# A mixture-of-experts stage: the last expert list as code of its own, its side work on DVE, and a deeper run ahead

## The reference

```python
def block_fn(args):
    tok, e = args                       # at most 128 rows of one expert
    xb = xf[tok]
    return (jax.nn.silu(xb @ w1[e]) * (xb @ w3[e])) @ w2[e]
...
y = y * gate_buf[:, None].astype(y.dtype)
out = jax.ops.segment_sum(y, tok_buf, num_segments=n)
...
e = jax.nn.sigmoid(h @ ple_gate_w[i] + ple_gate_b[i]) * (p[i] @ ple_w[i])
h = layer_norm(DEEPNORM_ALPHA * h + f + e, ln2_g[i], ln2_b[i])
```

## Time and profile before

| | |
|---|---|
| median of 3 runs | 2218.81 us (2215.59 to 2225.62) |
| the profiled execution | 2218.86 us |
| its span in the trace | 2217.1 us |
| instructions executed | 30503 |
| PE busy | 2142.3 us, 97% |
| PE weight loads busy | 1745.6 us, 79% |
| DVE busy | 1556.5 us, 70% |
| ACT busy | 1270.9 us, 57% |
| POOL busy | 175.5 us, 8% |
| 381 loads of expert chunks | 4.8 us each, median from issue to landing |

### The profile page before, as it was taken

One profiled execution on the slowest core, in us unless ns is written; L12 is line 12 of the kernel. 1 busy time (PEld: TensorE's weight loads), 2 busy tenths in 40 slices (PEclk: granted clock), 3 DMA queues, 4 the chain that ended last, 5 costly groups with the idle time before them and its releaser, 6 DMA issues.

```text
span 2217.1 us, 30503 instructions
## 1 busy us (share of the span) xinstructions
PE 2142.3 (97%) x11389; PEld 1745.6 (79%) x11389; DVE 1556.5 (70%) x1331; ACT 1270.9 (57%) x1270; POOL 175.5 (8%) x157
## 2 busy tenths in 40 slices
PE   9999999999999999999999999999999999999987
PEld 8977797877867999875777887878787878878765
DVE  6766544556246555635888888888888888888798
ACT  6755443333344333333677777676777776777655
POOL 0021010000202100200500000000000000000240
PEclk9999999999999999999999999999999999999999
DMA  6522594223835555543699999999999999999985
GB/s 224 185 95 91 178 349 158 71 76 115 262 128 198 182 186 190 161 148 114 233 406 360 376 367 370 377 361 369 368 366 369 368 357 380 365 370 368 357 321 230
DMA packets 85884, 584.56 MB, mean 264 GB/s; under 512 B 10016, under 2 KB 10016, under 8 KB 19504
## 3 DMA queue, kind: packets, MB, share of 16 engines
q1 hardware_dynamic: 76160, 547.91, 65.9%
q0 software_dynamic: 9184, 34.54, 4.4%
q10 hardware_dynamic: 464, 1.02, 0.1%
HBM read 563.06 MB, written 15.73 MB: 261 GB/s over the span
## 4 chain that ended last, share of the span: by engine, by line
PE 84%; DVE 6%; DMA 3%; ACT 2%; issue 2%; POOL 1%; ACTq 0%; POOLq 0%; DVEq 0%; SPq 0%
PE bank L582 75%; DVE wrest L2372 2%; DMA arena<-arena 2%; DMA ring<-in_w_moe 1%; PE bank L1294 1%; ACT whi L1737 1%; POOL arena L498 1%; PE bank L786 1%; PE bank L918 1%; PE bank L813 1%; DVE h L2123 1%; PE bank L1102 1%; PE bank L916 1%; PE bank L1120 0%; PE bank L895 0%
## 5 line engine op out<-in xcount | busy, mean ns | idle before, releaser
L2372 DVE TENSOR_TENSOR wrest<-ring,whi 128x2048 fp32r<-128x2048 f32 x381 | 869.9, 2331 | 97.0 <-ACT whi L1737 94.8
L1737 ACT ACTIVATE whi<-ring 128x2048 fp32r<-128x2048 f32 x378 | 703.8, 1918 | 83.7 <-DMA ring<-in_w_moe 81.3
L582 PE MATMUL bank<-whi,xgT 128*128 128x512 f32 x1008 | 406.7, 403 | 20.2 <-DVE wrest L2372 20.1
L582 PE MATMUL bank<-wrest,xgT 128*128 128x512 f32 x1008 | 397.2, 394 | 0.0
L582 PE MATMUL bank<-whi,xgR 128*128 128x512 f32 x1008 | 394.7, 392 | 0.0
L582 PEld LDWEIGHTS bank<-whi,xgT 128*128 128x128 f32 x1008 | 190.2, 189 | 66.7 <-DVE wrest L2372 26.5
L582 PEld LDWEIGHTS bank<-whi,xgR 128*128 128x128 f32 x1008 | 190.2, 189 | 47.1
L582 PEld LDWEIGHTS bank<-wrest,xgT 128*128 128x128 f32 x1008 | 189.5, 188 | 39.1
L582 PE MATMUL bank<-whi,hidE 128*128 128x512 f32 x504 | 201.3, 399 | 9.5 <-DVE hidR L2377 5.5
L582 PE MATMUL bank<-wrest,hidE 128*128 128x512 f32 x504 | 198.0, 393 | 0.0
L582 PE MATMUL bank<-whi,hidR 128*128 128x512 f32 x504 | 196.7, 390 | 0.0
(11 more groups left out here) (426 smaller groups left out, 3757.5 us busy)
## 6 DMA issues: line engine op xcount, KB each, us to landing
ring<-in_w_moe SPq DMA_DIRECT2D x381, 1024.0 KB, 4.8
ring<-in_w_dense SPq DMA_DIRECT2D x135, 1024.0 KB, 4.9
row<-in_rows POOLq DMA_DIRECT2D x17, 512.0 KB, 7.6
xg_rows<-ncT POOLq DMA_DIRECT2D x12, 512.0 KB, 20.4
y_rows<-arena POOLq DMA_DIRECT2D x9, 512.0 KB, 6.7
arena<-xg_rows SPq DMA_DIRECT2D x9, 512.0 KB, 5.4
arena<-arena POOLq DMA_DIRECT2D x32, 142.0 KB, 7.4
arena<-in_tbias POOLq DMA_DIRECT2D x2, 1536.0 KB, 16.3
```

What stands on the lines that cost most here:

```text
L582: ins = pe.matmul(out_, lhsT, rhs, start=start, stop=stop, **more)
L1737: S["w_hi"].on(a.activation(whi[:, n % HI_SLOTS, :], ring[:, c % RING, :], ACT.Copy))
L2372: S["w_lo"].on(v.tensor_tensor(wrest[:, s, :], ring[:, s, :], whi[:, n % HI_SLOTS, :].bitcast(F32), ALU.subtract))
```

## The change

The loop runs over all lists but the last (`last_list`, a value of its own in `plan_i`), and the last list follows as a second copy of the body, with `last` true: without `turn_gathered`, the split of gathered rows and the chunks ahead. In it DVE does POOL's weighting and adding, four operations at chunks 20, 24, 28 and 32, and PE takes its last chunk bank by bank, so that bank 2 is complete first. `hidE` and `hidR` have two buffers, and turn 6 stands between the two chunks of `second(5)`. `AHEAD` is 4. PE's wait for the copied outputs stands in step 1. `embed(1)`'s six operations each wait until PE has begun a given chunk of list 0.

```diff
-AHEAD = 3
+AHEAD = 4
+EMBED_AT, Y_AT = (4, 8, 12, 15, 18, 21), (20, 24, 28, 32)
...
+        hidE = (rounded("hidE0", 6144, 4, P), rounded("hidE1", 20736, 4, P))
+        hidR = (rounded("hidR0", 24064, 4, P), rounded("hidR1", 21248, 4, P))
...
-            for k in range(AHEAD):
-                sp.wait_ge(chunks_used.sem, n * E_CHUNKS + (N_DENSE - RING + k + 1))
-                s = (FIRST_SLOT + k) % RING
-                sp.dma_start(ring[:, s, :], w_moe[k]).then_inc(ready[s], 16)
...
+                    if i:
+                        pool.wait_ge(chunks_used.sem, N_DENSE + EMBED_AT[3 * j])
                     S["ple_done"].on(pool.tensor_tensor(fe[:, j, :], fe[:, j, :], ppx[:, j, :], ALU.mult))
...
-            pool.wait_ge(moe_dma, n_iter * 16 + (SCATTERED + 64))
-            for n in range(4):
-                S["m_fe"].on(pool.tensor_tensor(yg[:, n, :], yg[:, n, :], weight[:, n:n + 1].to_broadcast([P, D]), ALU.mult))
-            for n in range(4):
...
-                S["m_fe"].on(pool.tensor_tensor(fe[:, n % 2, :], fe[:, n % 2, :], yg[:, n, :], ALU.add))
...
+                def second(j, between=None):
+                    wait(pe, "m_hr", i * E_STEPS + (j + 1))
                     for half in range(2):
+                        if half and between is not None:
+                            turn_hid(between)
                         wh, wr = expert_chunk(i, n[0], 2)
                         n[0] += 1
+                        if last and j == E_STEPS - 1 and half:
+                            for c in range(2):
...
+                                S["m_w2"].on(ins)
...
-                    if j == 0:
-
+                    if j == 1:
                         wait(pe, "m_ya", i + 1)
                         wait(pe, "m_yv", i + 1)
                         wait(pe, "pg_in", 8)
-                    else:
+                    if j:
                         turn_hid(j - 1)
                     wait(pe, "m_hid", i * E_STEPS + j)
                     columns(1, "m_h3")
                     if j:
-                        second(j - 1)
-                turn_hid(E_STEPS - 1)
-                turn_gathered(i)
+                        second(j - 1, j if j == E_STEPS - 1 else None)
+                if not last:
+                    turn_gathered(i)
                 second(E_STEPS - 1)
...
+            with pe.Fori(0, last_list) as i:
+                expert_list(i, False)
+            expert_list(last_list, True)
...
                 wait(a, "m_tr", i * E_STEPS + (j + 1))
-                wait(a, "m_w2", i * E_STEPS + j)
+                wait(a, "m_w2", i * E_STEPS + max(j - 1, 0))
...
-                for n in range(AHEAD, E_CHUNKS + AHEAD):
+                for n in range(AHEAD, E_CHUNKS + (0 if last else AHEAD)):
                     round_chunk(i, n)
-                    if n == 3:
+                    if n == AHEAD:
                         copy_outputs(i)
...
+                    if last and n in Y_AT:
+                        q = Y_AT.index(n)
+                        if q == 0:
+                            wait(v, "ple_done", 12)
+                            v.wait_ge(moe_dma, last_list * 16 + (SCATTERED + 80))
+                        if q >= 2:
+                            v.wait_ge(S["m_fe"].sem, q - 1)
+                        S["m_fe"].on(v.scalar_tensor_tensor(fe[:, q % 2, :], yg[:, q, :], weight[:, q:q + 1], fe[:, q % 2, :],
+                                                            ALU.mult, ALU.add))
```

More of the change, by code:

```diff
@@ L1269, in _, with expert_list @@
             wait(pe, "router_done", 1)
-            n_iter = pe.value_load(plan_i[0:1, 0:1], min_val=N_EXP, max_val=LISTS)
+            last_list = pe.value_load(plan_i[0:1, 1 + SECONDS:2 + SECONDS], min_val=N_EXP - 1, max_val=LISTS - 1)
             assert over[0] == 1
-            with pe.Fori(0, n_iter) as i:
+            def expert_list(i, last):
                 n = [0]
@@ L1295, in turn_hid @@
                     S["m_tr"].on(ins)
-                def second(j):
-                    wait(pe, "m_hr", i * E_STEPS + j + 1)
+                def second(j, between=None):
+                    wait(pe, "m_hr", i * E_STEPS + (j + 1))
                     for half in range(2):
+                        if half and between is not None:
+                            turn_hid(between)
                         wh, wr = expert_chunk(i, n[0], 2)
                         n[0] += 1
+                        if last and j == E_STEPS - 1 and half:
+                            for c in range(2):
+                                cs = slice(c * 512, (c + 1) * 512)
+                                for k in range(2):
+                                    ins = split_product(ps[2 + c][:, :], (hidE[j % 2][:, 2 + k, :], hidR[j % 2][:, 2 + k, :]),
+                                                        (wh[:, k, cs], wr[:, k, cs]), False, k == 1)
+                                S["m_w2"].on(ins)
+                            give(1)
+                            continue
                         for k in range(2):
@@ L1781, in _ @@
                         round_hid(i, E_STEPS - 1)
-                        wait(a, "m_h3", i * E_STEPS + E_STEPS)
-                        round_gathered(i + 1)
-            copy_outputs(n_iter)
+                        if not last:
+                            wait(a, "m_h3", i * E_STEPS + E_STEPS)
+                            round_gathered(i + 1)
+            with a.Fori(0, last_list) as i:
+                expert_list(i, False)
+            expert_list(last_list, True)
+            copy_outputs(last_list, 1, E_STEPS)
         @block.vector
@@ L2440, in _, with expert_list @@
             prime(v, "m_hid", "m_hr")
-            with v.Fori(0, n_iter) as i:
-                for n in range(AHEAD, E_CHUNKS + AHEAD):
+            def expert_list(i, last):
+                for n in range(AHEAD, E_CHUNKS + (0 if last else AHEAD)):
                     rest_chunk(i, n)
-                    if n == 3:
+                    if n == AHEAD:
                         copy_outputs(i)
@@ L2452, in _ @@
                         rest_hid(i, E_STEPS - 1)
-                        rest_gathered(i + 1)
-            copy_outputs(n_iter)
-            wait(v, "m_fe", 8)
+                        if not last:
+                            rest_gathered(i + 1)
+                    if last and n in Y_AT:
[7 more added lines that the diff above has]
+                                                            ALU.mult, ALU.add))
+            with v.Fori(0, last_list) as i:
+                expert_list(i, False)
+            expert_list(last_list, True)
+            copy_outputs(last_list, 1, E_STEPS + 1)
+            v.wait_ge(S["m_fe"].sem, 4)
             layer_norm(fe, row_of("ln2_g", 3), row_of("ln2_b", 2), add_last)
```

47 lines of the change are left out of this document (23 added, 24 removed).

## The result

| | before | after |
|---|---|---|
| median | 2220.31 us (2215.59 to 2225.62, 6 runs) | 2193.4 us (2190.6 to 2201.66, 6 runs) |
| ratio | | 0.9885, 95% interval 0.9864 to 0.9907 |
| profiled execution | 2218.86 us, span 2217.1 | 2192.72 us, span 2191.0 |

The change makes the kernel 1.1% faster. The forecast was 2190.4, and the range of 2181 to 2203 holds the result.

What follows compares the result with a forecast made beforehand. PE, with 84% of the chain, bounds the kernel, so time is only where it stands still or does unneeded work. 2.3 + 8.3 + 5.1 + 1.4 + 8.4 + 3.0 = 28.5 off 2218.9 gives 2190.4 us; range 2181 to 2203.

Steps and rivals of the forecast that it cites:

- Turn 6: Usual list ends: turning ahead of chunk 39 with two buffers saves 0.25 us of the 0.77 lost, 2.3 us in all.
- R1: DVE doesn't hold chunk 40, or GpSimd costs nothing in list 0: 4.6 and 2.5 us more, both 2183; chance 0.15.
- Four ahead, waits moved: List borders: PE's waits at chunk 2 of the next list go, 8.3 us at seven borders and 5.1 at the last.
- the 1.67 of the last border: Chunks 2 to 11 after the last border: 1.67 us over their work, read as a clock below full after the wait.
- List 0: First list: PE turns 3.9 us earlier, less 2.5 charged for GpSimd's six embedding operations; net gain 1.4 us.
- The scatters: List 0: the four queue behind GpSimd's last embedding operation, with 38 us left for issue and landing; nothing charged.
- The price of one GpSimd operation: Beside DVE's subtractions: 2.0 us lost for each, kept against 3.4 by the Trainium skill's exclusion rule.
- R2: List 0: GpSimd shuts DVE out, so the embedding costs 11 us, not 2.5, and 2199 results; chance 0.17.
- The last list: Adds moved from GpSimd to DVE: of 10.97 us lost, 2.6 stay, so 8.4 us are gained.
- the transfers' part: Last list: waits for ring chunks landing beside the gather still cost PE 2.2 us, bounds 0.9 and 5.
- R3: Transfers are full: usual borders give nothing back and the last list keeps 5 us, giving 2204; chance 0.08.
- R4: Last list's own code comes late to PE: x us per chunk loses 42x, 2232 at x = 1.0; chance 0.04.

## Why the prediction was right

**The path.** The forecast sat on PE's waits and DVE's queue, and five of six terms came within 0.2 us. The sum is 0.7 below what was measured, and the dense stages took 3.07 longer: 2190.4 - 0.7 + 3.1 = 2192.8, where the profiled execution took 2192.72. That the forecast met the median to 3.0 us, with runs 11 us apart, says less.

**Turn 6.** Right in mechanism and size: DVE's queue, not the turn, was next in line, and kept over half of the loss at chunk 40: 0.28 a list went with the double buffer, 0.58 with hidR's place. R1 with its 4.6 more was wrong as a forecast of this kernel, but its 4.6 was there to be had, by an order of DVE that the change doesn't have: that run's eight usual lists gave 8 x 0.58 = 4.6.

**Four ahead, waits moved.** Right in sum. The prediction priced them together and thereby hid how unequal they are. Given the moved wait, the fourth chunk adds 1.27 at most. Without it, four ahead are 47 slower than the pair, and at 1161.53 they are 17.8 slower than the kernel before (1143.73), although all the rest of the change is in. The miss of that run, 2241.67 for "near 2220", is one of its expectation and not of the prediction: it had the wait right and left out the clock behind it. The prediction did read such a loss into the 1.67 of the last border and into list 0, and granted clocks of 0.87 (2069.42 to 2082.18) and 0.88 bear it out. But "after a wait of over 3 us" is no rule: a wait of 3.32 in the run with the wait in step 0 cost no clock, and one of 2.24 in the run with the adds on GpSimd cost 1.3 us and 0.3 more in the next round. The changed kernel kept its clock behind the same 2.24, and so did all four of the other variants with a wait of 2.25 there. The prediction charged nothing for it and gave no reason; that much was luck, worth 1.6 us.

**List 0.** The net of 1.4 was measured as 2.71 - 1.31 = 1.40, and the parts are nearly right by luck. Not foreseen was the 0.68 at chunk 2, behind bias additions of DVE that its fourth subtraction pushes back (with three ahead it is gone); the three waits sum to 3.32, where 1.3, 1.4 and 1.0 for GpSimd had been worked out at chunks 4 and 5. The charge for the first operation, 1.0, is shown by the run without spacing (2.24 to 1.24). The second cost nothing, where 0.9 was charged, and those at chunks 15 and 21 cost 0.77 and 0.68 (rounds of 17.85 and 17.76), where 0.2 each was charged: 2.45 in sum for 2.5. The scatters, charged at nothing, cost what they did before, only later: 18.34 for one round, 18.49 before.

**The price of one GpSimd operation.** 2.0 was near enough, but the reason for keeping it was wrong. DVE's and GpSimd's rows in list 0 of the changed kernel:

```profile
1090.98 3.52 DVE L2384 TENSOR_TENSOR wrest<-ring,whi 128x2048 fp32r<-128x2048 f32 x1 [1.30 <-ACT whi L1744]
...
1105.57 9.13 DVE L2384 TENSOR_TENSOR wrest<-ring,whi 128x2048 fp32r<-128x2048 f32 x4
...
1122.74 11.10 DVE L2384 TENSOR_TENSOR wrest<-ring,whi 128x2048 fp32r<-128x2048 f32 x4
```
```profile
1089.94 2.41 POOL L485 TENSOR_TENSOR arena<-arena 128x1024 f32<-128x1024 f32 x1 [46.65 <-PE bank L577]
1103.92 3.77 POOL L489 TENSOR_SCALAR arena<-h 128x1024 f32<-128x1024 f32 x1 [11.57 <-PE bank L577]
...
1123.83 3.46 POOL L485 TENSOR_TENSOR arena<-arena 128x1024 f32<-128x1024 f32 x1 [5.96 <-PE bank L577]
```

The first GpSimd operation ends at 1089.94 + 2.41 = 1092.35. DVE's subtraction is issued at 1090.98 and ends at 1094.50, a plain 2.2 behind that: DVE stood still for the rest of the operation. The later one starts while DVE is running, and takes 3.46 instead of 2.41; the four subtractions take 11.10 instead of 8.89. So about 1 us of its row is its own wait for DVE, and DVE loses 2.21, not 3.46. The Trainium skill (SBUF — State Buffer, "SBUF: two separate sides") says that of a DVE operation with two SBUF inputs and a GpSimd one that reads SBUF the one that starts first has the port for its whole instruction and the other blocks; for the tensor-tensor the rows agree. The prediction turned it down because it took 3.4, the whole row with GpSimd's own waits, for the time that DVE is shut out. (That the weightings' 3.4 holds such waits is argued from these rows: no trace has a weighting that runs alone.) R2's mechanism was thus right and its price was not: 11 us would have needed 3.4 from nearly each of the six, and only three cost anything.

**The last list.** The step that was off is "the transfers' part ... I take 2.2": it measured 1.05, near the lower bound of 0.9. The adds were charged 0.4 and cost 0.49; that "5.1 fits in two rounds" was a little off, as two rounds leave 2 x 2.5 = 5.0, but each add takes only 1.2 of DVE's time (2109.32 to 2110.51). The ring's loads beside the gather landed in 7.1 to 9.9 us, where the earlier trace rows has 7.6 to 10.4.

R3 is refuted by the usual borders, which gave back all that was forecast. The level that it leaned on, "366 to 370 GB/s, slice after slice", is 357 to 380 in rows 1, and the usual list now runs at 376. R4 is refuted by the rounds of 17.08 in the last list's own code (the run without adds), with no gap that lacks a releaser.

## What to carry over

Price each side of a pair alone before calling both good: here rounding one chunk further was worth 1.3 us at most with the wait moved, and with the wait where it had been the kernel came out slower than the one before. When a wait's producer is moved, look at what still stands in front of it in its own engine's queue, for the double buffer gave 0.28 a list until hidR also left its place behind a subtraction of 2.2. And a row of an engine that shares a resource contains its own waiting: take the lock's length from a row where that engine runs alone.

## What the hardware showed that I had not expected

- Behind most waits of 3.2 to 3.4 us, four chunks took 12.7 to 13.8 us at a granted clock of 0.80 to 0.87, so 1.6 to 2.7 us were lost on top of the wait. The length of the wait alone doesn't decide it: one of 3.32 was followed by a clock of 1.00, and the same wait of 2.24 at chunk 5 of list 0 by 1.00 in the changed kernel and by 0.66 in the run with the adds on GpSimd. What decides it stays open.
- GpSimd operations differ. A tensor-tensor beside DVE's subtractions costs them 2.21. The tensor-scalar, which reads SBUF too, costs them less: 9.13 - 8.89 = 0.24 above, and at most 1.0 in the run with the moved embedding, where two subtractions beside it took 5.48 for 4.49. It is stretched itself, from 2.78 to 3.77 and 4.63. By that rule of the Trainium skill (SBUF — State Buffer, "SBUF: two separate sides") it should shut DVE out as the tensor-tensor does; here the rows decide.
- The straight-line copy of the loop body has none of the two table loads of 1.28 us that every list's head has in the loop, and leaving the loop into it cost PE nothing that the rows show.
